# Feed-forward products with 512 columns per matmul, at another start address in each layer

## The reference, cut to what matters

```python
D_MODEL, SEQ, D_FF = 1024, 512, 2816

def conv_ffn(h, w_in, dw, w_out):                       # layers 0 and 1
    u = causal_dwconv(h @ w_in, dw)
    gate, val = u[..., :D_FF], u[..., D_FF:]
    return (jax.nn.silu(gate) * val) @ w_out

for layer in range(2):
    h = rmsnorm(x, norm_mix_g[layer])
    x = x + (rwkv7_time_mix(h, ...) if layer == 0 else conformer_conv(h, ...))
    x = x + memory_cross_attention(rmsnorm(x, norm_xattn_g[layer]), memn, ...)
    x = x + conv_ffn(rmsnorm(x, norm_ffn_g[layer]), ffn_w_in[layer], ffn_dw[layer], ffn_w_out[layer])
x = rmsnorm(x, final_norm_g)
# third layer: gated linear attention and FoX attention, then
a, val = jnp.split(rmsnorm_2(x, norm_ffn_g) @ w_up, 2, axis=-1)
a = causal_dwconv_2(a, conv_w, conv_b)
x = x + (jax.nn.gelu(a) * val) @ w_down
return rmsnorm_2(x, norm_final_g)
```

## Time and profile before

| | |
|---|---|
| runs (us) | 2565.75, 2565.78, 2570.45; median 2565.78 |
| profiled execution | 2563.58 us, its span 2561.8 us |
| mean granted TensorE clock | 0.989 |
| TensorE matmul busy | 2467.9 us (96%), 25275 records |
| VectorE / ScalarE / GpSimd busy | 1372.6 / 1135.6 / 993.9 us |
| chain of waits | PE 82%, DVE 8%, issue 6%, ACT 3% |

### The profile page before, as it was taken

How to read it: one execution, slowest core, us unless ns; L and a number is a source line. 1 busy time by engine, 2 the same in 40 slices (tenths; PEclk the granted TensorE clock), 3 DMA queues, 4 the chain that set the end, 5 groups by cost and what they waited for, 6 DMA issues and landing times.

```text
span 2561.8 us, 61987 instructions
## 1 busy us (share of the span) xinstructions
PE 2467.9 (96%) x25275; PEld 2330.1 (91%) x25275; DVE 1372.6 (54%) x2058; ACT 1135.6 (44%) x1677; POOL 993.9 (39%) x488
## 2 busy tenths in 40 slices
PE   7999898899999999998999999999999999999998
PEld 6888896897999999977989999999998769999998
DVE  7666554623577741798535777621153345555511
ACT  8844455544444432425535344433244454444422
POOL 3333220461444444325423444444443104444442
PEclk8899999999999999999999999999999999999999
DMA  4211001251333323323222333333222102323332
GB/s 151 82 59 59 1 1 64 91 189 36 97 98 98 98 99 107 124 66 110 88 66 67 99 98 98 99 107 116 90 92 72 44 1 92 99 97 98 99 101 73
DMA packets 62187, 219.54 MB, mean 86 GB/s; under 512 B 6752, under 2 KB 9184, under 8 KB 61408
## 3 DMA queue, kind: packets, MB, share of 16 engines
q1 hardware_dynamic: 58880, 207.76, 25.0%
q10 hardware_dynamic: 3168, 9.75, 1.1%
HBM read 213.29 MB, written 4.19 MB: 85 GB/s over the span
## 4 chain that ended last, share of the span: by engine, by line
PE 82%; DVE 8%; issue 6%; ACT 3%; POOL 1%; DVEq 0%; DMA 0%; POOLq 0%; ACTq 0%
PE psum L589 69%; DVE psum L2764 5%; PE psum L741 3%; PE psum L749 2%; PE psum L1102 1%; PE psum L1049 1%; PE psum L1292 1%; POOL wl L536 1%; PE psum L1331 1%; DVE psum L2335 1%; ACT wh L1424 1%; ACT psum L1454 0%; PE psum L1294 0%; PE psum L711 0%; PE psum L1319 0%
## 5 line engine op out<-in xcount | busy, mean ns | idle before, releaser
L536 POOL TENSOR_TENSOR wl<-raw,wh 128x1024 fp32r<-128x1024 f32 x388 | 947.8, 2452 | 1426.6 <-ACT wh L1424 1426.4
L589 PE MATMUL psum<-upl,wh 128*128 128x256 f32 x3696 | 729.7, 279 | 15.0 <-DVE upl L2855 7.4
L1424 ACT ACTIVATE wh<-raw 128x1024 fp32r<-128x1024 f32 x388 | 407.1, 1056 | 599.7 <-PE psum L589 576.7
L589 PE MATMUL psum<-uph,wh 128*128 128x256 f32 x3276 | 641.4, 277 | 4.6 <-DVE upl L2576 2.3
L589 PE MATMUL psum<-uph,wl 128*128 128x256 f32 x3276 | 638.9, 276 | 0.0
L589 PEld LDWEIGHTS psum<-upl,wh 128*128 128x128 f32 x3696 | 559.9, 188 | 27.9 <-issue 27.2
L589 PEld LDWEIGHTS psum<-uph,wh 128*128 128x128 f32 x3276 | 495.3, 188 | 7.2 <-DVE upl L2576 2.7
L589 PEld LDWEIGHTS psum<-uph,wl 128*128 128x128 f32 x3276 | 494.3, 188 | 0.0
L589 PE MATMUL psum<-hidh,wh 128*128 128x256 f32 x1056 | 209.6, 276 | 0.0
L589 PE MATMUL psum<-hidl,wh 128*128 128x256 f32 x1056 | 209.2, 276 | 0.0
L589 PE MATMUL psum<-hidh,wl 128*128 128x256 f32 x1056 | 209.1, 276 | 0.0
(11 more groups left out here) (477 smaller groups left out, 4480.4 us busy)
## 6 DMA issues: line engine op xcount, KB each, us to landing
raw<-in_weights SPq DMA_DIRECT2D x388, 512.0 KB, 3.4
xt<-in_x SPq DMA_DIRECT2D x4, 512.0 KB, 5.3
xt<-in_x ACTq DMA_DIRECT2D x1, 2048.0 KB, 8.3
out_x<-xt SPq DMA_DIRECT2D x6, 256.0 KB, 2.2
mem<-in_mem ACTq DMA_DIRECT2D x1, 1024.0 KB, 10.1
memn<-memh ACTq DMA_DIRECT2D x1, 1024.0 KB, 6.2
memn<-meml ACTq DMA_DIRECT2D x1, 1024.0 KB, 9.5
memh<-memn ACTq DMA_DIRECT2D x1, 1024.0 KB, 6.0
```

The source lines that it names most:

```text
L536: pool.tensor_tensor(wl[:, s, :], raw[:, s, :], wh[:, s, :].bitcast(F32), ALU.subtract).then_inc(split_done, 1)
L589: ins = pe.matmul(out[:, n:n + HALF], w, m[:, n:n + HALF], start=start and j == 0 and n == 0, stop=stop and j == 2 and n + HALF >= out.sha ...
L1424: act.activation(wh[:, s, :], raw[:, s, :], ACT.Identity).then_inc(split_hi, 1)
```

## The change

`product` gets a parameter `step`, which is 512 where the operand is one of the new feed-forward tensors and 256 elsewhere. These tensors exist once per layer at different addresses over the same memory: the input `ffnh[l]`/`ffnl[l]` begins 32, 128 and 256 bytes past a multiple of 512 in layers 0, 1 and 2, the hidden activations `hidh[l]`/`hidl[l]` 0, 480 and 384. The copies `firsth`/`firstl`, what makes them, their semaphores and the transpose ahead of tile 1 are gone. The loop over `up` tiles now takes tiles 1 to 40, the last three follow one by one. Everything else of the feed-forward parts is as before; the last output tile of `down2` still goes in halves of 256.

```diff
@@ -40,6 +40,8 @@
 HALF = 256
 PETAPS = 7
 ODD = 2
+FFN_AT = (0, 96, 224)
+HID_AT = (320, 288, 192)
 EPS = 1e-6
 LN_EPS = 1e-5
 GN_EPS = 64e-5
...
@@ -260,6 +262,8 @@
         cursor[0] += 16384 + 256
         uph, upl = (at("up" + n, [P, KT, T], F32R, act_at + 160 + 16384 * j) for j, n in enumerate("hl"))
         acth, actl = Placed(act_odd, ODD, uph), upl
+        ffnh, ffnl = ([at(f"ffn{n}{l}", [P, KT, T], F32R, act_at + FFN_AT[l] + 16384 * j) for l in range(3)]
+                      for j, n in enumerate("hl"))
         par = place("par", [P, NPAR + 6])
         eps = par[:, NPAR:NPAR + 6]
         common = place("common", [P, 3 * P])
...
@@ -352,10 +356,11 @@
 
 
         cursor[0] = zone
-        hidh, hidl = place("hidh", [P, FT, T], F32R), place("hidl", [P, FT, T], F32R)
+        hidh, hidl = ([at(f"hid{n}{l}", [P, FT, T], F32R, zone + HID_AT[l] + 2048 * FT * j) for l in range(3)]
+                      for j, n in enumerate("hl"))
+        cursor[0] += 4096 * FT + 512
         cu_at = cursor[0]
         cu = place("cu", [P, 4, T + 2])
-        firsth, firstl = (at("first" + n, [P, KT, T], F32R, zone + 49504 + 16384 * j) for j, n in enumerate("hl"))
         assert act_at % 512 == 32 and zone % 512 == 192
         cg, cv, sg = (place("ffn_" + n, [P, 2, T]) for n in ("cg", "cv", "sg"))
         acc_y, acc_x = (at("acc_" + n, [P, T], F32, cu_at + 8256 + 2048 * j) for j, n in enumerate("yx"))
...
@@ -579,16 +583,20 @@
             pe.sem_inc(sq_used, SC)
             pe.sem_inc(bonus_mm, SC)
 
-            def product(out, slot, b, hi, lo, start, stop, rows=slice(0, P), rest=1):
+            def product(out, slot, b, hi, lo, start, stop, rows=slice(0, P), rest=1, step=HALF):
 
                 w_h, w_l = wh[rows, slot, b * P:(b + 1) * P], wl[rows, slot, b * P:(b + 1) * P]
                 passes = [(w_h, hi), (w_l, hi)]
                 passes.insert(rest, (w_h, lo))
                 for j, (w, m) in enumerate(passes):
-                    for n in range(0, out.shape[1], HALF):
-                        ins = pe.matmul(out[:, n:n + HALF], w, m[:, n:n + HALF], start=start and j == 0 and n == 0,
-                                        stop=stop and j == 2 and n + HALF >= out.shape[1])
+                    for n in range(0, out.shape[1], step):
+                        ins = pe.matmul(out[:, n:n + step], w, m[:, n:n + step], start=start and j == 0 and n == 0,
+                                        stop=stop and j == 2 and n + step >= out.shape[1])
                 return ins
+
+            def columns(hi):
+
+                return T if any(hi is whole for whole in ffnh + hidh) else HALF
 
             def rest_at(hi, k):
 
...
@@ -1108,16 +1116,13 @@
 
             def ffn(l):
                 up, norm = f"up{l}", f"norm_ffn{l}"
-                tile(up, 0, norm, uph, upl)
+                tile(up, 0, norm, ffnh[l], ffnl[l])
                 norm_total(norm)
-                pe.wait_ge(first_hi, KT * (l + 1))
-                pe.wait_ge(first_lo, KT * (l + 1))
-                tile(up, 1, norm, firsth, firstl, behind_plain=True)
-                tile(up, 2, norm, firsth, firstl)
-                dense(up, norm, uph, upl, units=2 * FT - 4, skip=3)
-                tile(up, 2 * FT - 1, norm, uph, upl)
+                dense(up, norm, ffnh[l], ffnl[l], units=2 * FT - 4, skip=1)
+                for j in range(2 * FT - 3, 2 * FT):
+                    tile(up, j, norm, ffnh[l], ffnl[l])
                 if l < 2:
-                    down(f"down{l}", up, hidh, hidl)
+                    down(f"down{l}", up, hidh[l], hidl[l])
 
             def convolution():
 
...
@@ -1359,8 +1364,8 @@
                             split_unit(u)
                         if m == 0:
                             part("up2", k)
-                        mm = product(bank[(t0 + m) % 4], u % SLOTS, k % BLOCKS, hidh[:, k, :], hidl[:, k, :], k == 0,
-                                     k == FT - 1)
+                        mm = product(bank[(t0 + m) % 4], u % SLOTS, k % BLOCKS, hidh[2][:, k, :], hidl[2][:, k, :],
+                                     k == 0, k == FT - 1, step=T)
                         if k % BLOCKS == BLOCKS - 1 or k == FT - 1:
                             mm.then_inc(units_used, 1)
                 for h in range(2):
...
@@ -1526,11 +1531,6 @@
                             hold()
                             act.activation(sq[:, (n * s + j) % 2, :], x(i * 4 + s), ACT.Square,
                                            scale=pc(gain, i * 4 + s) if j else 1.0).then_inc(sq_ready, 1)
-                        if again:
-                            act.wait_ge(hi_ready, i * 4 + (g0 + s + 1))
-                            hold()
-                            act.activation(again[:, i * 4 + s, :], h[:, i * 4 + s, :].bitcast(F32),
-                                           ACT.Identity).then_inc(first_hi, 1)
                         weight_high(UNIT0[stage] + (s + 1) * per - 1 + SLOTS, i, 4 * per)
 
                 if isinstance(h, Placed):
...
@@ -2276,9 +2276,6 @@
                             dve.wait_ge(sq_ready, i * (4 * n) + (sq0 + n * s + j + 1))
                             dve.wait_ge(sq_used, i * (4 * n) + (sq0 + n * (s - 1) + j + 1 + SC))
                             dve.tensor_tensor(b[:, :], b[:, :], sq[:, (n * s + j) % 2, :], add).then_inc(sq_used, 1)
-                        if again:
-                            dve.wait_ge(lo_ready, i * 4 + (g0 + s + 1 + SC))
-                            dve.tensor_copy(again[:, k, :], l[:, k, :].bitcast(F32)).then_inc(first_lo, 1)
 
                 if isinstance(h, Placed):
                     half(0)
```

More of the change, by code:

```diff
@@ L616, in dense @@
                             mm = product(bank[(t0 + s) % 4][:, 0:n], (u0 + s) % SLOTS, k,
-                                         hi[:, k, 0:n], lo[:, k, 0:n], k == 0, k == KT - 1, rest=rest_at(hi, k))
+                                         hi[:, k, 0:n], lo[:, k, 0:n], k == 0, k == KT - 1, rest=rest_at(hi, k), step=columns(hi))
                         mm.then_inc(units_used, 1)
@@ L635, in tile @@
                     ins = product(bank[t % 4][:, 0:n], u % SLOTS, k, hi[:, k, 0:n], lo[:, k, 0:n],
-                                  k == 0, k == KT - 1, rest=rest_at(hi, k))
+                                  k == 0, k == KT - 1, rest=rest_at(hi, k), step=columns(hi))
                 ins.then_inc(units_used, 1)
@@ L656, in down @@
                             mm = product(bank[(t0 + s) % 4][:, :], (u0 + j) % SLOTS, k % BLOCKS,
-                                         hi[:, k, :], lo[:, k, :], k == 0, k == FT - 1)
+                                         hi[:, k, :], lo[:, k, :], k == 0, k == FT - 1, step=columns(hi))
                             if k % BLOCKS == BLOCKS - 1 or k == FT - 1:
@@ L1372, in last_down @@
                             split_unit(u)
-                        mm = product(bank[(t0 + KT - 1 + h) % 4][:, 0:HALF], u % SLOTS, k % BLOCKS, hidh[:, k, n],
-                                     hidl[:, k, n], k == 0, k == FT - 1)
+                        mm = product(bank[(t0 + KT - 1 + h) % 4][:, 0:HALF], u % SLOTS, k % BLOCKS, hidh[2][:, k, n],
+                                     hidl[2][:, k, n], k == 0, k == FT - 1)
                         if h and k == 2:
@@ L1504, in deltas, with deltas_normed @@
                         weight_high(UNIT0[stage] + skip + s + SLOTS, i)
[L1506 removed]
+            def deltas_normed(stage, per, norm, gain=None, h=acth):
                 x0, sq0 = plan(stage, "x"), plan(norm, "sq")
@@ L1897, in attention @@
                         act.activation(headh[:, j, :], tmp[:, (g0 + j) % 2, :], ACT.Identity).then_inc(hi_ready, 1)
-                deltas_normed(f"xo{l}", 1, f"norm_ffn{l}", h=uph, again=firsth)
+                deltas_normed(f"xo{l}", 1, f"norm_ffn{l}", h=ffnh[l])
             def ffn(l):
@@ L1914, in ffn @@
                         hold()
-                        act.activation(hidh[:, i * 2 + s, :], tmp[:, (g0 + s) % 2, :],
+                        act.activation(hidh[l][:, i * 2 + s, :], tmp[:, (g0 + s) % 2, :],
                                        ACT.Identity).then_inc(hi_ready, 1)
@@ L2185, in hybrid @@
                         sigmoids(2 * k + 6, 2 * k + 8)
-                deltas_normed("out2", 1, "norm_ffn2", h=uph, again=firsth)
+                deltas_normed("out2", 1, "norm_ffn2", h=ffnh[2])
             def last_norm():
@@ L2677, in attention @@
                 head_lows(3)
-                residual_normed(f"xo{l}", 1, f"norm_ffn{l}", ["norm_ffn_g"], [rstd], l * KT, uph, upl, again=firstl)
+                residual_normed(f"xo{l}", 1, f"norm_ffn{l}", ["norm_ffn_g"], [rstd], l * KT, ffnh[l], ffnl[l])
             def ffn(l):
@@ L2723, in ffn @@
                         dve.tensor_tensor(tmp[:, (g0 + s) % 2, :], sg[:, s, :], cv[:, s, :], mul).then_inc(val_ready, 1)
-                    lows(f"up{l}", hidh, hidl, i)
+                    lows(f"up{l}", hidh[l], hidl[l], i)
```

(4 more changed lines are left out.)

4 lines of the change are left out of this document (1 added, 3 removed).

## The result

| | before | after |
|---|---|---|
| median (us) | 2565.77 (2565.09 to 2570.45) | 2583.15 (2581.92 to 2587.32) |
| span of the profiled execution | 2561.8 | 2582.1 |
| mean granted TensorE clock | 0.989 | 0.989 |

The change makes the kernel slower: ratio 1.0072, 95% interval 1.0059 to 1.0085, +17.4 us between the medians. 2577 was forecast.

What follows compares the result with a forecast made beforehand. TensorE's matmul price was taken to bound the kernel; +12.7 (products) - 1.3 (slow tiles) - 0.3 (transpose) = +11.1 us on 2563.58 gave 2574.7, or 2577 against the median, range 2527 to 2598.

Steps and rivals of the forecast that it cites:

- TensorE bounds, and a product's price is the time: Feed-forward parts: each a single chain piece without a wait (359.53, 359.53, 347.58 us), so the matmul's cost sets the time.
- One product: 229.4 ns, 2.7 more than now: Up and down: each of 4686 wide products costs the midpoint of 226.7 and 232 ns, +12.7 us in all.
- the FoX rows: Forget-gate term of the FoX attention: 512-column fp32r matmuls at distance 0, behind plain matmuls, read as 232 ns each.
- the slow tiles: Tiles 1 and 2 of up0, reading the copies at 32 bytes past a multiple of 512: 117.8 ns per 256-column matmul.
- layer 0's piece: Layer 0's feed-forward chain piece of 359.53 us, holding 1560 of the products, should last 363.3 us.
- The -1.3 and -0.3: Up parts, us saved: -1.3 from tiles 1 and 2 no longer slow, -0.3 from the plain transpose ahead of them.
- They cost nothing now: Making the copies (24 casts on VectorE, as many copies on ScalarE) delays nothing, so dropping them brings nothing earlier.
- Rival A: Up and down: wide products make the kernel faster, in whole or in part of the layers; chance 0.33.
- The low bound in the sum, 4686 x -12.3 = -57.6 us: Up and down: lower limit for the 4686 wide products, 12.3 ns less each than now.
- The 64 ns for the last 128 columns: From earlier modelled durations: going from 384 to 512 columns adds 64 ns, while 256 to 384 adds 55.
- Rival B: No difference: operand streams at 0.443 ns a column however cut, 226.7 ns a product, -1.6 us, 2564; chance 0.20.
- Rival C: Up and down: without copies behind the plain matmul, slow pace everywhere, 235.6 ns a product, +40 us, 2606; chance 0.12.

Runs made afterwards that it cites:

- m2: e3 with 32 blocks of matmuls appended, each behind a plain matmul of growing width; 256 columns at 192 settled at 117.8 or 113.3 ns, 512 at 0 at 226.7.
- m1: e3 with blocks of 36 products appended, sweeping operand start, width and weight start; in 32-byte steps 512 columns cost 226.7 to 234.3 ns, 256 columns 113.3 to 120.0.
- e3: The changed kernel with feed-forward inputs at 256 and hidden activations at 0 in all layers, 512 columns; 2564.28 us, ratio 0.9998 to the kernel before.
- e4: e3 with two matmuls of 256 columns per feed-forward product instead of one of 512; 2626.54 us, ratio 1.0242 to the kernel before.
- e5: The kernel before, with tiles 1 and 2 of each up part reading the original at 192 instead of the copy; 2604.41 us, ratio 1.0151.
- e6: The kernel before with only the up and down products widened to 512 columns, copies and addresses kept; 2596.89 us, ratio 1.0125.
- e2: The changed kernel with all feed-forward operands 192 bytes past a multiple of 512, 512 columns, no copies; 2595.43 us, ratio 1.0114 to the kernel before.
- m3: e3 with blocks appended using 128, 64 and 32 columns of weights; 512 columns at 0 cost 226.7, 230.0 and 231.6 ns.
- b2: Against the kernel before: every full-width product 512 wide, every operand at 256 or 0, no copies, odd tiles or transposes ahead; 2629.25 us, ratio 1.0253.
- b3: b2 with the products ahead of the RWKV recurrence in 256 columns again, addresses kept; 2568.23 us, ratio 1.0018 to the kernel before.

## Why the prediction was right or wrong

*TensorE bounds, and a product's price is the time.* Right: the three pieces stayed whole and carry 18.5 of the 20.3 us.

*One product: 229.4 ns, 2.7 more than now.* The direction was right, the size was not: 4.2 ns, +19.5 us where +12.7 stood. The step that failed is "Down0 has the distance of the FoX rows, up0 that of the slow tiles; the other four stand in no row. I take the midpoint of 226.7 and 232." Down0, to which the FoX rows gave 232, came out at 226.7, and so did up2; the other four lie at 232.4 to 233.3, above the top of the two values averaged. The FoX products come singly between others, m2 shows 232 ns for the first five products at distance 0 and 226.7 afterwards, and m1's block with operand and weights both at 192, as in FoX, settles at 226.7 too: the row was right and most likely showed a start, not the settled pace of 500. For the same reason "so 512 cost about as much as two of 256 in the same place" fails at that distance once settled: 226.7 against 240.0 (e3, e4). The error at distance 0 (-5) and the one elsewhere (+4) partly cancel in the mean; layer 0's piece, forecast at 363.3 us, was 366.0. That the direction came out right is in part luck: the only 512-column row behind a price above 226.7 was one of distance 0, where a settled product costs 226.7, and the loss came from four other addresses, for three of which the prediction had no row.

*What goes, the copies, the other edits.* The -1.3 and -0.3 are too small to be told from the 1.8 us not placed. Down2's last row, taken at 0, costs its bound of +0.6. "They cost nothing now" holds for making the copies, but the text missed what reading them does: in 256 columns they are worth 39 us (e5). For the change this weighs nothing, since 512 columns at 192 cost 233.3 with them (e6) and without (e2).

*Rival A, faster, a chance of 0.33.* False: no stage and no block of m1 gave less than 226.7 ns for 512 columns. The low bound in the sum, 4686 x -12.3 = -57.6 us, is a term that no run shows: the lowest settled price is 226.7, as much as the pair of 256 before. A surplus made by the weight load, which a wide matmul would hide, is out by m3: with half the weight columns the surplus in 512 columns grows from 13.3 to 16.7 ns. A load does pace narrow matmuls (111.5 to 111.8 ns up to 192 columns, m1), but 256 columns lie past that floor, at 113.3 to 120.0 ns with 128, 64 and 32 columns of weights (m3). One wide matmul can carry less surplus than two narrow ones: at distance 0 it does, 13.3 ns less (e4 to e3), but the kernel before stood where two narrow ones cost 226.7 already. The 64 ns for the last 128 columns in the earlier trace rows are not the settled price either: at distance 0 that is 226.7 - 173.3 = 53.4 ns, the rate of 0.417 ns a column and nothing more, and at 192 it is 233.3 - 174.6 = 58.7 (m1); the row's 64 was most likely a start's too.

*Rival B, 0.20.* Its number, 226.7, is real at two of six stages and at all of e3's; its reason, a fixed rate a column, is not (m1's 320 columns).

*Rival C, 0.12.* 235.6 everywhere did not come, but four of six stages came within 3.2 ns of it. Its reason, the copies no longer there, is not the cause: e6 has them and is at 233.3.

## What to carry to other kernels

A baseline may stand at a favourable address by design or by luck: compare a new form with the old one at several addresses, not with the old one where it stands, or a gain of 62 us (e4 to e3) reads as nothing. Take a matmul's price from a long row of the same kind, past its first ten; a single one, or one block, shows a start or one of two paces (m2: about 232 ns for the first five to ten and 226.7 after them; 113.3 or 117.8 at 192). After any edit that changes the number of instructions ahead of a dense stage, look at that stage's waits for issue and its clock (64.3 us and 0.92 in b2, against 14.8 and 1.00 before) before blaming the edit's own products.

## What was not expected of the hardware

The price of an fp32r matmul changed with where its operand begins: in m1, with the weights at a multiple of 512 bytes, 226.7 to 234.3 ns for 512 columns and 113.3 to 120.0 for 256 in steps of 32 bytes, and the eight starts from 256 on repeated the eight below within 0.5 ns. Between these steps 512 columns cost 238.1 at 4 bytes and 236.8 at 240 (m1). With the weights moved, the six pairs tried in each width cost what the same difference of starts cost with unmoved weights, within 0.3 ns (m1). The width of the weights matters as well: with 64 columns of them 512 columns cost 230.0 to 230.9 at 0, 32 and 192 (m3). At distance 0 the price above 0.417 ns a column is 13.3 ns a matmul in 256, 320, 384 and 512 columns (16.0 in 448), at 192 it grows with the width, from 6.7 or 11.1 in 256 to 20.0 in 512 (m1). At 192, 256 columns have two stable paces, 113.3 and 117.8: eight blocks that differ in what stands ahead of them show both (m2), kv0 shows both behind the same instructions (e3, m1 to m3), and whether 96 matmuls of each up part read another address goes with the pace of the rest of it and of the down part (113.3 in before, 117.8 in e5). And 50 us of waits for issue, with 17 us more of busy time at a granted clock of 0.92 instead of 1.00, came and went with the width of the products ahead of an unchanged stage (b2, b3).
